# Score blocks and dense groups of the third branch's heads, in another order on TensorE

## The reference, cut to what matters

```python
def step(carry, inp):               # for one chunk of tokens
    b = jnp.cumsum(lb, axis=-1)
    dmat = jnp.where(tril, b[..., :, None] - b[..., None, :] + ib[..., None, :], -jnp.inf)
    ...
    w_ts = jnp.exp(dmat - m_t[..., None]) * jnp.einsum('bhtd,bhsd->bhts', qb, kb)
    num = dq[..., None] * jnp.einsum('bhtd,bhde->bhte', qb, C) + jnp.einsum('bhts,bhse->bhte', w_ts, vb)
    den = dq * jnp.einsum('bhtd,bhd->bht', qb, n) + jnp.sum(w_ts, axis=-1)
    h = num / jnp.maximum(jnp.abs(den), jnp.exp(-m_t))[..., None]
...
h = head_layer_norm(h, norm_w.reshape(H, d)).reshape(B, S, H * d)
return (h * jax.nn.sigmoid(o_pre.astype(f32))).astype(q.dtype)
```

## Time and profile before

| | us |
|---|---|
| median of 3 runs | 4439.3 (4424.22 to 4443.81) |
| the profiled execution, whole | 4428.86 |
| its span, first to last instruction | 4427.1 |
| PE busy | 4278.4 (97%) |
| DVE, POOL, ACT busy | 3092.1, 2817.6, 1800.0 |

### The profile page before, as it was taken

One profiled execution on the slowest core, in us unless ns is written; L12 is line 12 of the kernel. 1 busy time (PEld: TensorE's weight loads), 2 busy tenths in 40 slices (PEclk: granted clock), 3 DMA queues, 4 the chain that ended last, 5 costly groups with the idle time before them and its releaser, 6 DMA issues.

```text
span 4427.1 us, 74587 instructions
## 1 busy us (share of the span) xinstructions
PE 4278.4 (97%) x21290; PEld 3665.3 (83%) x21290; DVE 3092.1 (70%) x5263; ACT 1800.0 (41%) x3318; POOL 2817.6 (64%) x1633
## 2 busy tenths in 40 slices
PE   8999999999999999999999999999999999999998
PEld 6777876779999998788777778767899999978887
DVE  6666435647788667898866664366487887678988
ACT  4145123124576663333331550231245766533333
POOL 6843764765577666676668438647655776756665
PEclk9999999999999999999999999999999999999999
DMA  3233844734599999999822339448246999989997
GB/s 108 91 105 105 261 149 137 230 99 138 198 352 348 314 302 308 346 354 348 294 82 90 110 96 290 133 133 245 78 143 208 350 359 305 316 300 346 351 349 273
DMA packets 494913, 1011.86 MB, mean 229 GB/s; under 512 B 51536, under 2 KB 320464, under 8 KB 491856
## 3 DMA queue, kind: packets, MB, share of 16 engines
q1 hardware_dynamic: 420656, 739.77, 51.7%
q0 software_dynamic: 73728, 268.47, 17.0%
q10 hardware_dynamic: 288, 1.05, 0.1%
HBM read 846.57 MB, written 162.53 MB: 228 GB/s over the span
## 4 chain that ended last, share of the span: by engine, by line
PE 84%; DMA 4%; DVE 3%; ACT 3%; issue 3%; POOL 2%; SPq 1%; DVEq 0%; ACTq 0%; POOLq 0%
PE bank L1367 13%; PE bank L1424 7%; PE bank L1419 7%; PE pair L1020 7%; PE bank L1429 7%; PE bank L1371 6%; PE bank L1020 6%; PE pair L1022 4%; PE bank L1398 3%; PE bank L1046 3%; PE bank L1022 3%; PE pair L1046 2%; PE bank L1087 2%; PE pair L1087 2%; DMA ring<-u_tab 2%
## 5 line engine op out<-in xcount | busy, mean ns | idle before, releaser
L873 POOL TENSOR_TENSOR w_hi<-ring,ones 128x1024 fp32r<-128x1024 f32 x272 | 540.6, 1988 | 702.4 <-PE bank L1046 238.8
L1367 PE MATMUL bank<-xT,w_hi 128*128 128x384 f32 x2048 | 710.1, 347 | 5.4 <-ACT w_hi L1846 3.4
L876 POOL TENSOR_TENSOR w_lo<-ring,w_hi 128x1024 fp32r<-128x1024 f32 x272 | 692.9, 2548 | 21.4
L1367 PE MATMUL bank<-xl_peer,w_hi 128*128 128x384 f32 x2048 | 689.5, 337 | 0.0
L860 POOL TENSOR_TENSOR w_lo<-ring,w_hi 128x1024 fp32r<-128x1024 f32 x192 | 462.9, 2412 | 306.8 <-ACT w_hi L1846 305.8
L867 POOL TENSOR_TENSOR cl<-att,ch 128x384 fp32r<-128x384 f32 x256 | 376.5, 1471 | 327.4 <-ACT ch L1921 315.5
L1852 ACT CAST w_hi<-ring 128x1024 fp32r<-128x1024 f32 x252 | 265.4, 1053 | 665.8 <-PE bank L1429 465.3
L2724 DVE TENSOR_TENSOR w_lo<-ring,w_hi 128x1024 fp32r<-128x1024 f32 x252 | 342.2, 1358 | 121.5 <-ACT w_hi L1852 119.7
L1419 PE MATMUL bank<-w_hi,ch 128*128 128x512 f32 x1524 | 389.4, 391 | 12.6 <-ACT ch L1921 12.6
L1371 PE MATMUL bank<-xT,w_lo 128*128 128x384 f32 x2048 | 396.9, 334 | 0.0
L1367 PEld LDWEIGHTS bank<-xT,w_hi 128*128 128x128 f32 x2048 | 388.7, 190 | 6.8 <-issue 3.8
(11 more groups left out here) (404 smaller groups left out, 9416.1 us busy)
## 6 DMA issues: line engine op xcount, KB each, us to landing
ring<-v_tab SPq DMA_DIRECT2D x252, 512.0 KB, 7.0
ring<-w_stream SPq DMA_DIRECT2D x240, 512.0 KB, 3.8
g_spill<-gst SPq DMA_DIRECT2D x240, 192.0 KB, 4.6
vg<-w_spill SPq DMA_DIRECT2D x64, 704.0 KB, 10.2
att<-u_tab SPq DMA_DIRECT2D x320, 128.0 KB, 4.6
u_turned<-att SPq DMA_DIRECT2D x80, 512.0 KB, 5.6
ring<-u_tab SPq DMA_DIRECT2D x256, 128.0 KB, 3.6
ring<-u_turned SPq DMA_DIRECT2D x64, 512.0 KB, 5.6
```

Of the source, the lines that this page charges most:

```text
L873: nc.gpsimd.tensor_tensor(w_hi[b][:, 0:n], src, ones[:, 0:1].to_broadcast([P, n]), ALU.mult)\
L876: nc.gpsimd.tensor_tensor(w_lo[b][:, 0:n], src, w_hi[b][:, 0:n].bitcast(F32), ALU.subtract)\
L1367: nc.tensor.matmul(out, w_hi[s % 2][:, c * P:(c + 1) * P], dense_parts(c)[part], start=(c == 0 and part == 0), stop=False)
```

## The change

The score blocks of a round are issued in pairs, and a dense group of 6 matmuls (one `next(beside)`) follows each pair. The four groups that stood in one run of 24 matmuls behind the eighth block are the four that now stand among them; the rest of `share` is as before, so every round has the same 16 groups (8 in round 3) as before and the same matmuls. The waits are the same too, but the wait of `project_beside` for its slot 0 is reached behind the second score block, no longer behind the eighth.

```diff
-                def scores_of(i, p):
-                    for s in (2 * p, 2 * p + 1):
-                        pe.wait_ge(drained_sem[s], drnd(L, "MQ", i) + 2)
-                    for s in range(TT):
+                def scores_of(i, p, blocks):
+                    if 0 in blocks:
+                        for s in (2 * p, 2 * p + 1):
+                            pe.wait_ge(drained_sem[s], drnd(L, "MQ", i) + 2)
+                    for s in blocks:
                         b = 4 + s % 2
                         fill_wait(b, L, "MQ", i, 2 * p + s // 2)
...
                     if i < 3:
                         beside = project_beside(L, "MQ", i + 1, x_parts(xl_mix), 6)
-                        share = [4, 2, 2, 2, 2, 2, 2]
+                        share = [1, 1, 1, 1, 2, 2, 2, 2, 2, 2]
                     else:
                         beside = project_beside(L, "MC", 0, x_parts(xl_mix), 6, range(2))
-                        share = [4, 1, 1, 1, 1, 0, 0]
+                        share = [1, 1, 1, 1, 1, 1, 1, 1, 0, 0]
...
-                    scores_of(i, 0)
-                    scores_of(i, 1)
-                    dense()
+                    for p in range(2):
+                        for blocks in ((0, 1), (2, 3)):
+                            scores_of(i, p, blocks)
+                            dense()
```

## The result

Median of 20 runs each: 4431.82 us before, 4444.45 us after, ratio 1.003 with a 95% interval of 1.0023 to 1.0038, so 10 to 17 us slower. The profiled execution of the changed kernel has a span of 4434.8 us, that of before 4427.1. In a later set of runs the same two kernels gave 4433.8 and 4457.06 us (ratio 1.005, 1.0031 to 1.0069; only six runs of the changed kernel, two near 4443 us and four from 4456 to 4462).

What follows compares the result with a forecast made beforehand. PE's own sequence bounds the kernel (84% of the last chain). Per layer -2.02 + 1.86 + 1.7 + 1.8 + 1.7 - 0.8 = +4.2 us, +8.5 for two, on median 4439.3: 4447.8 us; 8-in-10 range 4425 to 4459.

Steps and rivals of the forecast that it cites:

- The waits between blocks: Round 0, first score block to first numerator: PE's waits for DVE's products vanish, 12.16 to 10.14 us, gaining 2.02.
- changes of kind: PE's passages between score blocks and dense matmuls: four per segment after the change, 0.36 us together.
- Rival 3: Passages between fp32 scores and dense matmuls are dear: at 0.3 us each 14.4 us on top, 4462 us; chance 0.09.
- The wait for the split: Rounds 1 and 2, first dense group: PE stands 3.9 us for POOL's slot 0 weights; loses 1.86 and some 1.8 us.
- Rival 2: Slot 0 is split in time in rounds 1 and 2: 14 us faster in all, 4425.3 us; chance 0.11.
- The clock: Rounds 1 and 2, behind PE's new wait: PE's granted clock falls, costing 1.7 us more each, bounds 0 and 1.85.
- rival 1: PE's clock stays up behind the 3.9 us wait, which costs only itself: sum +1.7, 4441.0 us; chance 0.25.
- Round 3: Slot 0 is ready before the scores; DVE's later last block limits the gain to 0.8 us, not 1.66.
- In rounds 0 to 2 the same lateness stays covered: DVE's later last block costs nothing there: dense groups and the second head's products lie between; PE wants bank 7 later.
- The sum: All gains and losses of the rounds added: +4.2 us per layer, +8.5 us over two layers.
- The number: Forecast time of the whole changed kernel: 8.5 us on the median of the runs, 4439.3, gives 4447.8 us.

Runs made afterwards that it cites:

- the kernel with the splits first: Changed kernel, but POOL splits slots 0 and 1 ahead of rewriting `sel` in the held-up rounds; 4426.43 us against 4429.65 before, ratio 0.9999.
- the half with rounds 1 and 2 alone: Changed kernel with the new order only in rounds 1 and 2, rounds 0 and 3 as before; 4445.45 us against 4429.65 before, ratio 1.0044.
- the half with rounds 0 and 3: Changed kernel with the new order only in rounds 0 and 3, the others as before; 4426.52 us against 4429.65 before, ratio 0.9994.
- both edits: Changed kernel with POOL's splits ahead of `sel` and DVE's variance ahead of its first turn; 4425.53 us against 4435.04 before, ratio 0.9973.
- all three edits: Changed kernel: POOL's splits first, DVE's variance first, fourth dense group behind first numerator and denominator; 4425.18 us against 4435.04 before (0.9981), later 4420.08 against 4433.8.

## Why the prediction was right, and where its steps were not

**The waits between blocks** (forecast -2.02 us a round): -2.3 in both layers' round 0. The segment takes 9.90 us, not 10.14; the four changes of kind cost 0.12 us in all, not 0.36. Rival 3, dear changes of kind, is out: in the kernel with the splits first seven segments without a wait, each with three more passages in each direction than before, took 9.86 to 9.91 us.

**The wait for the split** (forecast 3.9 us of idle, 14.09 us to the numerator): 3.73 us in all four places of the first trace, and 13.90 us where the clock stayed up. It costs 1.67 us a round net of the block waits it replaces; forecast 1.86. Rival 2 is out: splitting first removed the wait and moved the loop by 21 us, and the half with rounds 1 and 2 alone carries the loss.

**The clock** (forecast 1.7 us a round, rival 1 had it at nothing): over the changed kernel's two traces and the half with rounds 1 and 2, twelve places in all, the segment took 13.9 us in two and 15.2 to 16.7 in ten; the mean excess over 13.9 is 1.74 us (0 to 2.8). Rival 1 is out as the usual case. The size was right, though one row under it was misread: PE's wait behind the loop was 4.20 us, not some 4.7 (PE's timeline has its last matmul before it at 809.78 and `[4.20 <-POOL w_lo L876]` on the one at 814.37). That the fall differs from place to place was not said. The Trainium skill (TensorE: Matmul & The Clock Gate, section "Why this matters for your kernels") warns of idle gaps between bursts of matmuls; the traces agree in ten of twelve.

**Round 3** (forecast -0.8 us): this step failed. With nothing else late it lost 0.6 and 0.9 us (the half with rounds 0 and 3). The step had DVE's lateness right (it took the last block 10.5 us behind the start of the first, where it had been 8.3) but took the divide at its length before; beside POOL's split of slot 2 its second instruction takes 2.0 us, not 0.69, and that split begins earlier in the round because slot 0 is done earlier. These 1.3 us are nearly the whole distance between the gain of 0.8 and the loss of 0.6 in the first layer. In the second layer the loss is the price of the clock behind the new waits, a term that the step put at nothing. It also missed bank 6: ACT's numerator, which frees it, waits for the same divide, and PE's second numerator waits 1.04 us for ACT. In the changed kernel itself round 3 came to -0.65, -0.2, -0.8 and +1.2 us: there the scores began at full clock, behind waits of 0.55 to 1.48 us instead of 2.31, and only the last of the four places, the first layer of the first trace, had the clock fall behind the mean's wait (2.01 us, then 0.74 over 4 us). That two of them lie near the forecast is in part luck, since the full clock at the start was no part of it.

**"In rounds 0 to 2 the same lateness stays covered"**: this failed too, in rounds 1 and 2. The second mean waits for the variance, 1.79, 0.56, 1.65 and 1.48 us (1.98, 1.33, 1.54 and 0.73 in the second trace). The prediction had looked at the queue of SP for late ring loads, found them covered, and left out that the same queue feeds the transfer that DVE's next turn waits for, with the variance, a mask and so PE behind it. In part this lateness replaces another: where PE waited for the variance, the wait at the end of the round became shorter or vanished, since ACT's chain had run on meanwhile.

**The sum** (forecast +8.5 us in the loop): +10.9 and +11.7 in two pairs of traces, +12.6 timed. Over both layers and in the order of the two pairs: round 0 gave -4.6 and -4.6 us (forecast -4.0); rounds 1 and 2 up to the first numerator gave +12.0 and +14.0 (forecast +14.1, the clock in it +5.4 and +7.3 for 6.8); behind the numerator they gave +2.9 and +3.1 (forecast 0, the covered lateness); round 3 gave +0.4 and -0.9 (forecast -1.6). So the missing 2 to 3 us are the lateness that was not covered, and part of round 3.

**The number** (forecast 4447.8 us, measured 4444.45) is closer than its parts: the base of three runs was 7.5 us above the median of twenty, and the loss was forecast 4.1 us too small, and the two errors have opposite signs. The loss itself, 8.5 forecast and 12.6 timed, is the fairer comparison.

## What to carry to other kernels

Before moving work forward into a gap, ask of its operands when they are ready, not only whether the gap is long enough: here two rounds out of four had their weights 3.7 us too late, for a reason that stood on another engine, and one entry of a list decides it per round. When an engine becomes late by a microsecond, follow every instruction behind it in its queue that waits for a transfer, since a transfer turns a small delay into the wait of whatever stands next; here moving that next one only handed the wait on. Look also at what the late engine then runs beside: 1.3 us of round 3 came from one product that had met POOL's split. And a gain of 10 us in a program whose other stages vary by 20 is read from the stage's own length in the trace, and from many runs.

## What the runs showed of the hardware that was not expected

**DVE and POOL wait for one another in some instructions.** The same 128x512 product of two SBUF operands on DVE took 0.69 us alone and 2.00 us beside POOL's `w_lo` of a slot; a decay mask of the same size took 0.69 us alone and 0.82 to 2.64 us beside a split. The length follows from one thing: in the loops of the fourteen traces 180 such products and masks began while POOL was splitting, and every one ended 0.54 to 0.56 us behind the end of the POOL instruction that was running. In the pair shown for round 1, POOL ended at 683.16 + 2.35 = 685.51 and DVE at 686.06. So the product takes as long as POOL still needs, and then 0.55 us, which looks like waiting its turn and not like a slower rate. It goes the other way too: POOL's `w_lo`, 2.35 us beside nothing and also in that pair, where it was first, took 2.72 us in the kernel before at 699.60, where it began while a decay mask that had waited (698.58, 1.48 us) was still running. Not every DVE instruction was held: beside `w_lo` the reciprocal took its 3.34 to 3.36 us, the turn its 1.23 to 1.25, and the 128x512 products with one operand in PSUM their 0.65 to 0.69.

**The clock's fall behind an idle stretch of PE was not certain.** Behind 3.73 or 3.74 us it stayed at 1.00 in two of twelve identical places, and in the two low ones shown above it was 0.74 over the next 5.6 us and 0.72 over the next 6.0. Behind 2.31 to 2.38 us it fell at the end of round 2 in all four places of the two traces of the kernel before, in four of six places with both edits, and in none of twelve in the two traces with all three edits. What decides it the runs do not show.
